# Index keys loaded as 2 KB rows, the sample's pieces seven gathers apart, tile 0's value rows split by stage, one pair of heads routed ahead of the first gather

## The chip, the cores and the metric

The kernel runs on one core of one Trainium2 chip. The metric is the device time of one execution in microseconds (us), smaller is better. The engines are named as in the profile: PE (TensorE, with PEld for its weight loads), DVE (VectorE), ACT (ScalarE), POOL (GpSimd) and SP (SyncE). SP does no computing here: it issues the large loads to 16 shared DMA engines.

## What is computed

One step of a decoder layer, for a prompt of 528 rows (16 meta tokens and 512 tokens) and a sample group of 8 sequences with 8 new tokens each, in float32. The parts that matter here:

```python
# every token: one projection, then two attentions
I[t, s] = IDX_SCALE * sum_h w[t, h] * relu(q_idx[t, h] . k_idx[s])    # 4 heads of 64: the token indexer
sel     = top_k(I, 256)                                             # sample: over 2048 cached keys and 8 new ones
y_a     = attention(q_a, k_a[sel], v_a[sel])                        # sparse
y_b     = softmax(q_b . k_b / 8 + forget bias) @ v_b                # over all keys; the sample's lie in pages
h = LN1(ALPHA * x + w_out(sig(g_a) * (y_a @ W_a) + sig(g_b) * (y_b @ W_b)))
# product-key experts: 8 heads x 16 of 16384 experts for each token
pre  = u[expert] . h ;  coef = softmax(top) * gelu(pre) ;  out = sum coef * v[expert]
x = LN2(ALPHA * h + out)
```

The caches lie in pages of 128 keys, in a random order that a page table gives, 16 pages for each of the 8 sequences. Each expert row (u or v) has 1024 floats, 4 KB.

## The kernel before

The program has three phases, with a barrier of all engines after each of the first two. Phase 1 (`project`) makes the projection. Phase 2 (`prompt`) computes both attentions of the prompt, and with them, in step order (`merge_at`), the merge, the output projection and the first norm of tile 0 (the tiles of tokens for the experts are 0 to 3 for the prompt, 128 tokens each, and 4 for the 64 sample tokens). Phase 3 is everything else, and its order is a written plan.

**The plan.** The backbone is the list `gathers` (L434 to L447): 1152 indirect loads that POOL issues (L820). Each brings one expert row for each of 128 tokens, 512 KB, from `peer_u` (v = 0) or `peer_v` (v = 1) into one of 10 row buffers (16 from gather 750 on). Numbered from 0, the first 256 are tile 0's, u in 0 to 127 and v in 128 to 255; then 64 u rows of tile 1; from 320 on u and v of different tiles alternate. Before POOL issues gather n it waits until the row that was in this buffer (row n - 10) has been read. POOL issues in order, so one unread row holds all gathers behind it. Before every 32nd u row of a tile it waits for that pair of heads to be routed (`pair_routed`).

Every other piece of phase 3 is put at a gather number (`put(n, ...)`), and `plan` is the merged list. PE, ACT and DVE each walk through the same plan in order and do what is theirs. A row counts as work of the engine that reads it: all u rows are read by DVE (L1860, a multiply and sum); v rows either by DVE (L1867, L1869, scale and add) or by PE (L1214, products with a diagonal of coefficients that ACT makes in `spot`, L1512, four gathers ahead). `read_by_dve` (L449) says which: of tile 0's v rows three in four are DVE's, of tiles 1 to 3 one in eight.

What is placed around the change:
- `route` (L1794): for one tile and one pair of heads g, four stages on DVE that find the top 16 experts. For tile 0 the pairs g = 0 and 1 stand in `pre_items`, ahead of gather 0; g = 2 at gathers 4 to 16, g = 3 at 20 to 32.
- `merge_items(1)`: the merge and output projection of tiles 1 to 3 (gathers 0 to 112), their norms, then 16 `query` products on PE (L1069) at gathers 128 to 176, three gathers apart, and the key `score` products (L1081) up to gather 187.
- `sample_items` (L487), from gather 190 on: `ix` c (L1103, products of the index queries `qis` with the index keys of stage c: c = 0 to 3 are 512 keys of each sequence, c = 4 the new ones) and `iy` c (L1116, the weighted sum over heads). `ix` 0 is at gather 191, `iy` 0 at 194, and after a gap of 48 `ix` 1 at 242, `ix` 2 at 245, `ix` 3 at 250. Then eight rounds q of the sample's attention (q < 4 are the k_b, v_b rounds, q >= 4 the sparse ones), each with scores (L1150), a softmax (`s_max`, `s_exp`, `s_norm`, `s_turn`) and `s_weigh` (L1190), five gathers between pieces for q < 4. Beside them 32 `top` rounds on DVE (L1733) pick the 256 keys. They all end at gather 726; tile 4's merge ends at 806, and L548 asserts that this is below 830.
- SP's own order: `prompt` (L681) issues stores and the first merge weights; `first_merges` the weights of `query`; `sample` (L718) the index keys (128 loads, stage 0 of all sequences first, then after `sc_ready` 16, the last key scores, stages 1 to 3 sequence by sequence), then the pages of k_b, v_b and kv_a into a ring of four slots, each when its slot has been read. Page numbers come from a table in SBUF (`page_numbers`), so SP also runs register instructions between the loads.

The index keys of one page are 64 rows (one per feature) of 128 keys:

```python
            sp.dma_start(ring[s_][p0:p0 + 64, at + j % 4 * 128:at + (j % 4 + 1) * 128],   # L730: 64 rows of 512 B
```

so that `ix` contracts over 128 partitions, two sequences at a time, and the queries of a sequence must stand on its 64 partitions in `qis`. DVE copies them there with 16 small copies and the new keys with 2 (L1602 to L1615) at the end of phase 1.

## Time and profile before

| | us |
|---|---|
| median of 3 runs | 2494.94 (2492.96 to 2496.37) |
| the profiled execution | 2496.61 |
| its span, first to last instruction | 2494.8 |
| PE busy | 1870.8 (75%) |
| DVE busy | 1664.1 (67%) |
| POOL busy | 1344.5 (54%) |
| ACT busy | 433.0 (17%) |
| granted TensorE clock, mean | 0.879 |

The core's DMA engines moved 791.69 MB, 604.58 MB of them on POOL's queue (the gathers) and 180.59 MB on the queue of SP and ACT. The first gather is issued at 466.9 us, the last at 2474.3 us. Times below count from the first instruction. "Releaser" in brackets is what ended an engine's idle time. "DMA share" is the mean busy share of the 16 DMA engines; the trace shows values up to 1.04 where they are full. A row of windows gives start:end and length, the busy time and number of instructions of PE, PEld, DVE, ACT and POOL, then the granted clock, the DMA share and GB/s.

### The profile page before, as it was taken

The page shows a single profiled execution, that of the slowest core. Times are in us where ns is not written, and L with a number is a line of the kernel's source. Part 1 is how long each engine was busy: PE and PEld are TensorE (multiplying, and loading weights), DVE is VectorE, ACT ScalarE, POOL GpSimd, SP SyncE. Part 2 cuts the span into 40 slices and gives each one's busy share as a digit, 9 for nine tenths or more (in the row PEclk, how much of TensorE's full clock was granted, in tenths as well). Part 3 has the DMA queues.
Part 4 walks back from the last instruction along what each step waited for, and adds up shares of the span by engine and source line. Part 5 has one row for each costly group of instructions (what it writes and reads, how often), then busy time and mean ns, then how long its engine had stood idle before and what let it go on. Part 6 is the DMA issues. An engine that isn't in the chain of part 4 may idle for free. (4 is left out here: it accounts for less than half of the span.)

```text
span 2494.8 us, 23480 instructions
## 1 busy us (share of the span) xinstructions
PE 1870.8 (75%) x6566; PEld 909.3 (36%) x6566; DVE 1664.1 (67%) x3371; ACT 433.0 (17%) x1052; POOL 1344.5 (54%) x1174
## 2 busy tenths in 40 slices
PE   8999998979759736326767677667678986667686
PEld 6756644735335412102222223233234542222231
DVE  2114886798784997987997575489555469745544
ACT  0123533101011201101111022122121121111110
POOL 1100000357755656655445467756767668877775
PEclk9998987989979868659887899889889998899999
DMA  4205330889989989999999999989999999899997
GB/s 182 63 12 168 96 119 9 314 319 386 409 293 340 317 253 385 402 396 348 377 381 350 367 381 380 390 326 358 400 405 409 409 397 344 332 372 410 408 394 294
DMA packets 258180, 791.69 MB, mean 317 GB/s; under 512 B 30562, under 2 KB 55203, under 8 KB 257347
## 3 DMA queue, kind: packets, MB, share of 16 engines
q0 software_dynamic: 166400, 604.58, 63.4%
q1 hardware_dynamic: 90692, 180.59, 20.6%
q10 hardware_dynamic: 960, 5.03, 0.5%
q8 instruction: 54, 0.88, 0.1%
q14 instruction: 74, 0.61, 0.1%
HBM read 783.90 MB, written 5.59 MB: 316 GB/s over the span
## 5 line engine op out<-in xcount | busy, mean ns | idle before, releaser
L1214 PE MATMUL ps<-arena 128*128 128x512 f32 (+1 forms) x1600 | 845.4, 664 | 310.5 <-DMA arena<-peer_v,arena 263.5
L820 POOL DMA_INDIRECT arena<-peer_u,arena x576 | 671.9, 1167 | 610.5 <-DVE arena L1823 317.7
L1860 DVE CUSTOM_DVE_ANT_0 arena<-arena 128x1024 f32<-128x1024 f32 x576 | 694.0, 1226 | 394.3 <-DMA arena<-peer_u,arena 385.7
L820 POOL DMA_INDIRECT arena<-peer_v,arena x576 | 653.2, 1134 | 390.0 <-PE ps L1214 178.0
L1214 PEld LDWEIGHTS ps<-arena 128*128 128x128 f32 (+1 forms) x1600 | 300.0, 203 | 798.6 <-issue 628.0
L1869 DVE SCALAR_TENSOR_TENSOR arena<-arena 128x1024 f32<-128x1024 f32 x171 | 219.9, 1286 | 128.9 <-DMA arena<-peer_v,arena 124.1
L1512 ACT ACTIVATE arena<-arena 128x128 f32<-128x128 f32 (+1 forms) x400 | 149.4, 394 | 728.5 <-PE ps L1214 725.1
L1037 PE MATMUL ps<-arena 128*128 128x448 f32 (+2 forms) x512 | 158.0, 468 | 22.6 <-DVE arena L1763 21.9
L1069 PE MATMUL ps<-arena 128*128 128x128 f32 (+2 forms) x768 | 149.4, 354 | 3.0 <-ACT arena L1400 3.0
L849 PE MATMUL ps<-arena 128*128 128x296 f32 (+1 forms) x512 | 130.7, 415 | 10.5 <-DMA arena<-w_proj 10.5
L1190 PE MATMUL ps<-arena 128*64 128x512 f32 (+1 forms) x512 | 90.7, 501 | 61.3 <-DMA arena<-v_b 61.3
L1069 PEld LDWEIGHTS ps<-arena 128*128 128x128 f32 x768 | 111.1, 198 | 44.4 <-issue 10.4
L1037 PEld LDWEIGHTS ps<-arena 128*128 128x128 f32 x512 | 89.4, 194 | 95.8 <-issue 79.8
L849 PEld LDWEIGHTS ps<-arena 128*128 128x128 f32 (+1 forms) x512 | 95.8, 188 | 43.8 <-issue 12.1
L1150 PE MATMUL ps<-arena 128*32 128x512 f32 x256 | 47.7, 881 | 81.3 <-DMA arena<-k_b 73.2
L804 POOL DMA_INDIRECT arena<-logf_b,arena x16 | 14.6, 912 | 129.6 <-PE ps L849 129.6
L1190 PEld LDWEIGHTS ps<-arena 128*64 128x64 f32 x512 | 36.3, 150 | 122.4 <-issue 121.7
L1733 DVE MAX8 arena<-arena 64x8 f32<-64x2056 f32 x32 | 73.6, 2300 | 1.2
L885 PE MATMUL ps<-arena 64*128 64x384 f32 (+9 forms) x168 | 70.5, 529 | 3.7 <-ACT arena L1376 1.9
L1734 DVE MATCH_REPLACE8 arena<-arena 64x2056 f32<-64x2056 f32 x32 | 73.1, 2286 | 0.0
L1049 PE MATMUL ps<-arena 128*128 128x512 f32 (+1 forms) x128 | 56.7, 596 | 1.8 <-DVE arena L1763 1.8
L1168 PE MATMUL ps<-arena 128*128 128x128 f32 x128 | 23.7, 362 | 42.3 <-ACT arena L1471 42.2
(192 smaller groups left out, 1648.7 us busy)
## 6 DMA issues: line engine op xcount, KB each, us to landing
arena<-k_b SPq DMA_DIRECT2D x128, 256.0 KB, 20.8
arena<-v_b SPq DMA_DIRECT2D x128, 256.0 KB, 15.4
arena<-w_mix SPq DMA_DIRECT2D x56, 512.0 KB, 6.7
arena<-w_q SPq DMA_DIRECT2D x48, 512.0 KB, 6.6
arena<-kv_a SPq DMA_DIRECT2D x128, 128.0 KB, 15.1
arena<-w_out SPq DMA_DIRECT2D x24, 512.0 KB, 6.7
arena<-peer_u,arena POOLq DMA_INDIRECT x576, 9.1
arena<-peer_v,arena POOLq DMA_INDIRECT x576, 6.8
```

The lines of the kernel that those rows point to most:

```text
L820: pool.indirect_dma_start(out=rows[slot_of[n]], out_offset=None, in_=io["peer_v"] if v else io["peer_u"], in_offset=bass.IndirectOffsetOnA ...
L849: last = pe.matmul(bank(2 * (m % 2) + a, HT, 0, n), wring[m % 3][:, k, 0:n], xT[:, k, a * HT:(a + 1) * HT], start=(k == 0), stop=(k == KD ...
L885: last = pe.matmul(out, heads[0:rows_, q, q0:q0 + nq], heads[0:rows_, kt, c0:c1], start=True, stop=not biased)
L1037: last = pe.matmul(out, mw_k[u % NMW][:, k0 + k, :], src[:, k, :], start=(k == 0), stop=(k == nk - 1))
L1069: last = pe.matmul(bank(4 + n % 2, WIDTH[p]), mw_k[u % NMW][:, k, :], hT[p][:, k, :], start=(k == 0), stop=(k == KD - 1))
L1190: last = pe.matmul(out[e], probT_s[:, c, j * 128 + 64 * e:j * 128 + 64 * e + 64], rhs, start=(c == 0 and j == 0), stop=False)
L1214: last = pe.matmul(bank(6 + a, 512, 0, nt), diag_p[read_before[n] % ND][:, 0:nt], rows[slot_of[n]][:, a * 512:(a + 1) * 512], start=(k == ...
L1512: act.activation(diag_p[r_ % ND][:, 0:nt], place, ACT.Copy, scale=coef[i % 2][:, k:k + 1]).then_inc(dp_ready, 1)
L1733: step(dve.max(top8, isamp))
L1734: step(dve.match_replace(isamp, top8, isamp, TAKEN))
L1860: dve.tensor_tensor_reduce(out=row, in0=row, in1=h, scale=1.0, scalar=0.0, op0=ALU.mult, op1=ALU.add, accum_out=pre[:, k:k + 1]).then_inc( ...
L1869: ins = dve.scalar_tensor_tensor(facc, row, c, facc, ALU.mult, ALU.add)
```

## The change

It makes five edits.
1. `kidx` pages are loaded as 16 rows of 2 KB (4 features of 128 keys each) onto 16 partitions of a sequence. `ix` then contracts over 64 partitions, four sequences at a time, in four accumulating steps r, so it has 8 matmuls for each c instead of 4.
2. The queries and new keys for that form no longer come from DVE's copies. SP stores them to DRAM (5 stores, pieces of 32 B) in phase 2, ahead of its stores of v and k, waits for that, and loads them back with 16 small loads ahead of the fifth merge weight.
3. Tile 0's v rows: k < 16 three in four on DVE as before, k = 16 to 63 all on DVE, k = 64 to 127 every second on DVE (92 rows on DVE instead of 96).
4. Tile 0's routing: only pair 0 ahead of gather 0; pair 1 at gathers 2 to 11, pair 2 at 16 to 28, pair 3 at 34 to 46; the gate at 52 and 56, and `gelu` and `coefs` of tile 0 not before 57 and 60.
5. Sample plan: the gap after `iy` 0 is 22 instead of 48 (`ix` 1 at gather 216, `ix` 2 at 219, `ix` 3 at 224, `ix` 4 at 229); pieces of q < 4 seven gathers apart instead of five; the gap after `s_out` for q >= 3 is 8 instead of 16. The sample's part ends at gather 738, tile 4's merge at 818.

```diff
@@ -335,11 +335,12 @@
         idx_added, mask_ready, weights_ready = sem("idx_added"), sem("mask_ready"), sem("weights_ready")
         pt_ready, pt_copied = sem("pt_ready"), sem("pt_copied")
         o_ready, o_copied = sem("o_ready"), sem("o_copied")
-        spread_a, spread_d = sem("spread_a"), sem("spread_d")
+        spread_a = sem("spread_a")
         wrow_spread, wd_ready = sem("wrow_spread"), sem("wd_ready")
         lidx_ready, lp_loaded, lf_ones = sem("lidx_ready"), sem("lp_loaded"), sem("lf_ones")
         g0_ready, g0_copied, sig0_done = sem("g0_ready"), sem("g0_copied"), sem("sig0_done")
         b0_ready, b0_mixed, ln0_loaded = sem("b0_ready"), sem("b0_mixed"), sem("ln0_loaded")
+        qsc_stored, qsc_loaded = sem("qsc_stored"), sem("qsc_loaded")
         ix_ready, ix_read, iy_ready, iy_read = (sem(n) for n in ("ix_ready", "ix_read", "iy_ready", "iy_read"))
         tail_new = sem("tail_new")
         masks_ready, rows_loaded = sem("masks_ready"), sem("rows_loaded")
@@ -363,6 +364,7 @@
         folded = sem("folded")
 
         csc = nc.dram_tensor("neg_cumulative", [NH, T], F32, kind="Internal").ap()
+        qsc = nc.dram_tensor("index_of_sample", [64, NB, NI + 1, SN], F32, kind="Internal").ap()
 
         def col(j, w=1, p=128, p0=0):
             return small[p0:p0 + p, j:j + w]
@@ -452,7 +454,7 @@
             if i == 4:
                 return k % 2 == 0
             if i == 0:
-                return k % 4 != 3
+                return k % 4 != 3 if k < 16 else k < 64 or k % 2 == 0
             return k % 8 == 5
 
         by_dve = [read_by_dve(*g) for g in gathers]
@@ -485,22 +487,22 @@
             return out
 
         def sample_items():
-            out = [(("zero",), 0), (("spread", 0), 1), (("ix", 0), 3), (("iy", 0), 48), (("ix", 1), 3)]
+            out = [(("zero",), 0), (("spread", 0), 1), (("ix", 0), 3), (("iy", 0), 22), (("ix", 1), 3)]
             for c in range(2, 5):
                 out += [(("ix", c), 2), (("iy", c - 1), 3)]
             out += [(("iy", 4), 2), (("admit",), 1)]
-            out += [(("s_score", 0, c), 5) for c in range(5)]
+            out += [(("s_score", 0, c), 7) for c in range(5)]
             out += [(("s_max", 0), 2), (("s_exp", 0), 2), (("s_norm", 0), 2), (("s_turn", 0), 3)]
             for q in range(NB):
                 if q + 1 < NB:
                     out.append((("spread", q + 1), 0))
-                g = 5 if q < 4 else 3
+                g = 7 if q < 4 else 3
                 if q < 3:
                     for c in range(5):
-                        out += [(("s_score", q + 1, c), 5), (("s_weigh", q, c), 5)]
+                        out += [(("s_score", q + 1, c), 7), (("s_weigh", q, c), 7)]
                 else:
                     out += [(("s_weigh", q, c), g if c < 4 else 1) for c in range(5)]
-                    out += [(("s_out", q), 16)]
+                    out += [(("s_out", q), 8)]
                     if q + 1 < NB:
                         out += [(("s_score", q + 1, c), 3) for c in range(5)]
                 if q + 1 < NB:
@@ -509,12 +511,13 @@
             return out
 
         pre_items = [item for item, _ in merge_items(0)]
-        pre_items += [("route", 0, g, s_) for g in range(2) for s_ in range(4)]
+        pre_items += [("route", 0, 0, s_) for s_ in range(4)]
         for s_ in range(4):
-            put(4 + 4 * s_, "route", 0, 2, s_)
-            put(20 + 4 * s_, "route", 0, 3, s_)
-        put(38, "gate_in", 0)
-        put(42, "gate", 0)
+            put(2 + 3 * s_, "route", 0, 1, s_)
+            put(16 + 4 * s_, "route", 0, 2, s_)
+            put(34 + 4 * s_, "route", 0, 3, s_)
+        put(52, "gate_in", 0)
+        put(56, "gate", 0)
 
         at = 0
         for item, gap in merge_items(1):
@@ -554,8 +557,8 @@
             for g in range(-(-rows_of[i] // 32)):
                 k1 = min(32 * g + 32, rows_of[i])
                 n = gather_at[i, 0, k1 - 1]
-                put(max(n + 3, 44 if i == 0 else 0), "gelu", i, g)
-                put(max(n + 6, 47 if i == 0 else 0), "coefs", i, g)
+                put(max(n + 3, 57 if i == 0 else 0), "gelu", i, g)
+                put(max(n + 6, 60 if i == 0 else 0), "coefs", i, g)
         for n, (i, v, k) in enumerate(gathers):
             if not by_dve[n]:
                 put(max(n - 4, gather_at[i, 0, min(32 * (k // 32) + 32, rows_of[i]) - 1] + 7), "spot", n)
@@ -684,17 +687,28 @@
                                  csc[:, LP + b * SN:LP + (b + 1) * SN]).then_inc(tail_new, 16)
                 for w in range(NMW):
                     weights(w)
+                for h in range(NI + 1):
+                    sp.dma_start(qsc[:, :, h, :], heads[0:64, QI + h, LP:T].rearrange("p (b t) -> p b t", t=SN)
+                                 ).then_inc(qsc_stored, 16)
                 for i, (t0, nt) in enumerate(TILES):
                     sp.dma_start(io["v_out"][t0:t0 + nt, :], vtm[0:nt, i, :]).then_inc(v_stored, 16)
                 sp.dma_start(io["k_out"][:, 0:2, :], heads[0:64, KA:KA + 2, :]).then_inc(k_stored, 16)
                 sp.dma_start(io["k_out"][:, 2:3, :], heads[0:64, KI:KI + 1, :]).then_inc(k_stored, 16)
                 sp.dma_start(io["k_out"][:, 3:11, :], heads[0:64, KB:KB + NH, :]).then_inc(k_stored, 16)
                 x_rows(0)
+                sp.wait_ge(qsc_stored, 16 * (NI + 1))
+                for b in range(NB):
+                    c0 = b % 4 * 32
+                    of_b = qsc.rearrange("(p r) b h t -> b p r h t", r=4)[b]
+                    sp.dma_start(qis[16 * b:16 * b + 16, :, c0:c0 + 32], of_b[:, :, 0:NI, :].rearrange("p r h t -> p r (h t)")
+                                 ).then_inc(qsc_loaded, 16)
+                    sp.dma_start(kin[16 * b:16 * b + 16, :, :], of_b[:, :, NI, :]).then_inc(qsc_loaded, 16)
                 for w in range(NMW, first_query + NMW):
                     weights(w)
                     if w == weight_no["out", 0, NMW, 0]:
                         for dst, l in ((lng0, 0), (lnb0, 1)):
                             sp.dma_start(dst, io["ln"][l:l + 1, :].partition_broadcast(128)).then_inc(ln0_loaded, 16)
+                sp.wait_ge(qsc_loaded, 16 * 2 * NB)
                 sp.wait_ge(k_stored, 16 * 3)
                 sp.wait_ge(tail_new, 16 * NB)
 
@@ -724,12 +738,11 @@
                         sp.wait_ge(mix_done, KD)
                     for b in range(NB):
                         nos = page_numbers(b * NPG + 4 * c0, 4 * (c1 - c0))
-                        p0, at = 64 * (b % 2), b // 2 * 512
                         for j, no in enumerate(nos):
                             s_ = c0 + j // 4
-                            sp.dma_start(ring[s_][p0:p0 + 64, at + j % 4 * 128:at + (j % 4 + 1) * 128],
-                                         io["kidx"].rearrange("(n d) k -> n d k", d=64)[bass.ds(no, 1)].rearrange(
-                                             "o d k -> (o d) k")).then_inc(ring_loaded[s_], 16)
+                            sp.dma_start(ring[s_][16 * b:16 * b + 16, j % 4 * 512:(j % 4 + 1) * 512],
+                                         io["kidx"].rearrange("(n p r) k -> n p (r k)", p=16, r=4)[bass.ds(no, 1)].rearrange(
+                                             "o p x -> (o p) x")).then_inc(ring_loaded[s_], 16)
                 for z, (kind, q, c, e) in enumerate(fill_list):
                     s_ = z % NSLOT
                     if kind == "ki":
@@ -1097,12 +1110,14 @@
                 if c >= 2:
                     pe.wait_ge(ix_read, 2 * (c - 1))
                 w = 512 if c < 4 else SN
-                keys = unit("ki", -1, c, 0).rearrange("p (a n) -> p a n", a=4) if c < 4 else kin
-                for g in range(2):
-                    for p in (2 * g, 2 * g + 1):
-                        last = pe.matmul(bank(2 * (c % 2) + g, w), qis[:, p, :], keys[:, p, :], start=(p % 2 == 0),
-                                         stop=(p % 2 == 1))
-                    last.then_inc(ix_ready, 1)
+                keys = unit("ki", -1, c, 0).rearrange("p (j r k) -> p r j k", j=4, r=4) if c < 4 else kin
+                for r_ in range(4):
+                    for g in range(2):
+                        p0 = 64 * g
+                        last = pe.matmul(bank(2 * (c % 2) + g, w), qis[p0:p0 + 64, r_, :], keys[p0:p0 + 64, r_],
+                                         start=(r_ == 0), stop=(r_ == 3))
+                        if r_ == 3:
+                            last.then_inc(ix_ready, 1)
                 if c < 4:
                     pe.wait_ge(ix_ready, 2 * c + 2)
                     pe.sem_inc(slot_read, 1)
@@ -1599,20 +1614,6 @@
                 for g in range(NKV):
                     dve.tensor_copy(qac[64 * g:64 * g + 64], heads[0:64, QA + 4 * g:QA + 4 * g + 4, LP:T])
                     dve.tensor_copy(kan[64 * g:64 * g + 64, :], heads[0:64, KA + g, LP:T])
-                dve.wait_ge(zero_set, 1)
-                for h in range(NI):
-                    for e in range(2):
-                        for pp in range(2):
-                            c0 = (2 * pp + e) * 32 + h * 8
-                            dst = qis.rearrange("p (a b) c -> p a b c", b=2)[64 * e:64 * e + 64, :, pp, c0:c0 + 8]
-                            src = heads[0:64, QI + h, LP:T].rearrange(
-                                "p (a b e t) -> p a b e t", b=2, e=2, t=SN)[:, :, pp, e, :]
-                            dve.tensor_copy(dst, src)
-                for e in range(2):
-                    last = dve.tensor_copy(
-                        kin[64 * e:64 * e + 64, :, :],
-                        heads[0:64, KI, LP:T].rearrange("p (a e t) -> p a e t", e=2, t=SN)[:, :, e, :])
-                last.then_inc(spread_d, 1)
 
             norms = [0]
```

## Rows read from the trace of the kernel before

**Rows 1.** Windows of the span: busy time, then PEclk, DMA share, GB/s.

```profile
467.00:590.00 123.00, 105.03 (x303) 56.15 (x302) 115.44 (x310) 14.47 (x32) 78.69 (x63) 0.93 0.93 345
...
730.00:835.00 105.00, 104.37 (x348) 60.54 (x347) 59.30 (x88) 15.77 (x36) 58.94 (x54) 1.00 0.97 349
835.00:940.00 105.00, 50.99 (x99) 18.93 (x97) 100.93 (x245) 11.46 (x29) 65.55 (x51) 0.70 0.86 278
940.00:1110.00 170.00, 75.91 (x263) 25.45 (x263) 148.96 (x192) 20.30 (x39) 112.65 (x90) 0.68 1.04 398
1110.00:1200.00 90.00, 61.27 (x203) 23.81 (x201) 68.04 (x150) 16.41 (x36) 40.91 (x38) 0.87 0.92 344
...
1300.00:1420.00 120.00, 78.45 (x251) 28.42 (x251) 77.98 (x101) 18.52 (x40) 55.94 (x50) 0.77 0.93 346
```

**Rows 2.** What POOL waited for, 730 to 835 us: total, times, longest.

```profile
POOL arena L820 <- PE ps L1214: 33.6, 13, 7.2
```

**Rows 3.** What POOL waited for, 835 to 940 us.

```profile
POOL arena L820 <- DVE arena L1869: 27.5, 12, 4.1
```

**Rows 4.** From the page's costliest groups: busy us, mean ns | idle before.

```profile
L1869 DVE SCALAR_TENSOR_TENSOR arena<-arena 128x1024 f32<-128x1024 f32 x171 | 219.9, 1286 | 128.9 <-DMA arena<-peer_v,arena 124.1
```

**Rows 5.** Timeline of DVE: first and last instruction of one routed pair.

```profile
450.99 0.49 DVE L1783 MAX8 arena<-arena 128x8 f32<-128x128 f32 x2 [24.31 <-ACT arena L1414]
...
465.97 0.20 DVE L1823 SCALAR_TENSOR_TENSOR arena<-arena 128x32 uint32<-128x32 f32 x1
```

**Rows 6.** Gathers of line L820: from issue to landing.

```profile
DMA to landing us min/median/max: 4.2/7.6/24.1
```

**Rows 7.** Timeline of PE: start us, us, what [idle before <-releaser].

```profile
820.42 1.88 PE L1214 MATMUL ps<-arena 128*128 128x512 f32 x4
...
844.03 3.68 PE L1103 MATMUL ps<-arena 128*128 128x512 f32 x8 [2.50 <-DMA arena<-kidx]
...
949.20 5.10 PE L1103 MATMUL ps<-arena 128*128 128x512 f32 x8 [3.92 <-DMA arena<-kidx]
```

**Rows 8.** Timeline of SP's queue: all index key loads; those of stages 1 to 3.

```profile
802.97 145.76 SPq L730 DMA_DIRECT2D arena<-kidx  x128
...
845.87 102.86 SPq L730 DMA_DIRECT2D arena<-kidx  x96
```

**Rows 9.** SP's issues by line: ns min/median/max, first and last start.

```profile
L730 SPq DMA_DIRECT2D arena<-kidx x128: 468/469/602, 803.0 to 948.3; - x128
...
L743 SPq DMA_DIRECT2D arena<-k_b x128: 332/333/2527, 952.7 to 1374.5; - x128
...
L683 SPq DMA_DIRECT2D arena<-neg_cumulative x8: 263/295/298, 201.5 to 203.9; - x8
```

**Rows 10.** Windows of line L820 alone: x is the number of gathers issued.

```profile
466.00:881.50 415.50, 263.48 (x216) 0.90 0.94 344
466.00:909.00 443.00, 279.52 (x228) 0.89 0.93 339
466.00:962.00 496.00, 314.69 (x257) 0.87 0.93 336
```

**Rows 11.** What PE waited for, 940 to 1850 us.

```profile
PE ps L1150 <- DMA arena<-k_b: 73.2, 9, 16.2
PE ps L1190 <- DMA arena<-v_b: 61.3, 11, 11.0
```

**Rows 12.** SP's DMA queue, 835:940 and 1000:1080: packets, MB, share.

```profile
q1 hardware_dynamic: 7134, 2.93, 11.5%
...
q1 hardware_dynamic: 5587, 10.18, 33.8%
```

**Rows 13.** What DVE waited for at the first barrier: us, times, longest.

```profile
DVE arena L1633 <- PEq L636: 35.0, 1, 35.0
```

**Rows 14.** Timeline of SP's queue in the prompt phase.

```profile
212.43 21.92 SPq L671 DMA_DIRECT2D arena<-w_mix  x6
```

**Rows 15.** Timeline of PE there: the product with the fifth merge weight.

```profile
228.70 5.29 PE L904 MATMUL ps<-arena 128*128 128x128 f32 x32
```

## The prediction, made before the changed kernel was run

> **What bounds the kernel now.** I read the windows of the span first. From the first gather on, the DMA engines are the common bound: where they are full their share is 1.04, and a window below that holds idle DMA time of (1.04 - share) x length [rows 1]. That gives 13.5 us in 467 to 590, 7.4 in 730 to 835, 18.9 in 835 to 940, none in 940 to 1110, 10.8 in 1110 to 1200 and 13.2 in 1300 to 1420. Only such time can be won: the bytes of the gathers do not change. Next I asked who left the engines idle. In 730 to 835 POOL waits 33.6 us for rows that PE has not read, and PE is busy 104 of 105 us [rows 1, 2]: the `query` products stand in its path. In 835 to 940 POOL waits 27.5 us for DVE's reads, DVE is busy 101 of 105 us, and PE half the time [rows 1, 3]. A read of a v row costs DVE 1.29 us [rows 4].
>
> **Routing pair 1 behind gather 0: 0.** The first gather waits for pair 0 alone in both kernels. Routing a pair takes DVE 15.2 us [rows 5]. Before, pair 1 fills the time in which the first rows land; behind the change DVE waits for them, some 6 us (a gather lands 4.2 us after its issue at best, 7.6 in the median [rows 6]), and the work of pair 1 still comes. DVE is busy 115 of 123 us here [rows 1], so this is a loss. The gain is that the last pair ends at gather 46 instead of 32: fourteen more rows are asked for sooner, while DVE reads (1.29 us) faster than full DMA engines deliver (90 gathers in 170 us, 1.9 us each [rows 1]), worth at most 14 x 0.6 = 8 us. I take 0, with -8 and +7 as ends.
>
> **Rows 144 to 191 all on DVE.** A row costs PE 1.88 us [rows 7]. Eleven PE rows (147, 151, up to 187) go before the last key score: -21 us of PE's path, of which at most the window's 7.4 us of idle DMA time is gained on the gathers. DVE has room: 59 of 105 us busy [rows 1], and twelve reads more are 15 us. **Rows 192 to 255 half on DVE.** DVE, the bound of 835 to 940, loses nine reads (rows 193 to 225), 9 x 1.29 = 12 us, within that window's 18.9 us. So far this is a gain of up to 19 us at gather 256, if nothing else stands there.
>
> **The index keys: where it goes wrong.** Something does stand there: `ix` 1 moves from gather 216 + 26 = 242 to 216, and PE, which walks the plan in order, waits in it until stage 1 of the keys has landed. Before, it waits only 3.9 us, until 949.2 us [rows 7]. When will they land now? SP issues the 128 loads in an unbroken run of 145.8 us, the 96 of stages 1 to 3 in 102.9 us [rows 8], so 1.07 us a load, of which the load instruction itself is 0.47 [rows 9]; the rest is register work for page numbers, which the change keeps. The loads interleave the stages, so stage 1 ends about when the whole does. The new load (16 rows of 2 KB) has no row. Its issue lies between 0.26 us, the least of the 8-row loads, and 0.47, today's; nearest in kind is 0.33, rows of 2 KB too [rows 9]. With 0.33, 0.14 us a load is saved. The start: four of PE's eleven removed rows stand ahead of the query that lets SP begin, -7 us; 32 loads of stage 0, -4.5; and SP no longer waits 2 us for the last key score: -13 in all. Then 88 loads to the end of stage 1, -12. Stage 1 lands at 949.2 - 25 = 924 us (915 with 0.26, 940 with 0.47).
>
> But row 215 was issued just before 881.5 us [rows 10] and comes no later now; I take 870 and landing at 876. From there PE stands still for 48 us. Half of the v rows from 192 on are now PE's, so row 217 stays unread, and gather 227, which takes its buffer, is held, with all behind it. DVE's removed work gains nothing then. After 924 PE runs `ix` 1. Today's four matmuls take 3.7 us, or 5.1 at a lower clock [rows 7]; eight take 7.4 to 10 if each costs the same, I take 9; then row 217, and gather 227 goes out at about 935. Before, 228 gathers were out by 909 [rows 10]: 27 us late. The next 29 take 53 us before (257 by 962 [rows 10]). Now the DMA engines start empty, but `ix` 2 and 3 (7.4 us each) stand between the next PE rows: I take 51 us. So gather 256 is 25 us late, with 16 and 41 from the two issue costs, and everything after it shifts. The 7 and 12 us above are in this, not beside it.
>
> The doubled matmuls are the uncertain piece within it. The Trainium skill (TensorEngine Tiling, Theoretical Speedup) has a contraction of 64 or less run up to twice as fast in two row tiles, and the two halves here use different partitions. By that rule `ix` stays at 3.7 to 5.1 us and the total would be some 4 us lower than by the row; no row here shows two such halves side by side.
>
> **Seven gathers between pieces.** Between 940 and 1850 PE waits 73.2 us for k_b and 61.3 us for v_b [rows 11], and while it waits its v rows hold POOL. A piece consumes 2 MB. SP's queue gets a share of 0.34 of the engines beside full gathers [rows 12], about 127 GB/s, so five gathers (5 x 1.9 us, from 90 gathers in 170 us [rows 1]) bring 1.2 MB and seven 1.7 MB: PE waits less. But while PE waits the loads themselves keep the engines busy, so the 134 us of waiting are worth only the idle DMA time of those windows, 10.8 + 13.2 us, and part of that is the softmax turn between rounds, which stays. I take half of the sum and less for the later rounds: -11 us, ends 0 and -24. The shorter gap after `s_out` fits in work that stays full: 0.
>
> **2 KB rows.** Keys in 512 B rows: 2.93 MB in 0.115 x 105 = 12.1 us of all engines, 243 GB/s. k_b in 2 KB rows: 10.18 MB in 0.338 x 80 = 27 us, 377 GB/s [rows 12]. 4.19 MB of keys take 17 us and would take 11. These 6 us fall into the stall, so they are 0 here; if there is no stall they count.
> The Trainium skill (DMA: Bandwidth & Descriptors, Specifications) gives 512 B as the least transfer at line rate; by that the 6 us don't exist, against the rows here.
>
> **The detour of the queries.** DVE's 18 copies lie in front of a barrier at which DVE waits 35.0 us for PE [rows 13]: removing them gains 0. SP's queue in phase 2 gets five stores of 512 pieces of 32 B (0.26 to 0.6 us each by the issues shown [rows 9], more if the pieces count, for which there is no row), a wait until they have landed (4 us, as the quickest gather [rows 6]), and 16 small loads of 0.26 to 0.47 us: 10 to 15 us together. All of it stands ahead of the fifth merge weight, issued at 212.4 us [rows 14]: it goes out at 222 to 227 and lands 4 to 8 us later [rows 6], 226 to 235. PE begins with it at 228.7 us [rows 15]. PE is busy most of that phase, so I count +4 us, ends 0 and +10. If a whole step's slack covers it, it costs nothing.
>
> **The sum** is made against the profiled execution: 2496.6 + 0 + 25 - 11 + 4 = 2514.6 us. The median of the runs is 1.7 us below that execution, so I predict **2513 us**. A difference of 0.2%, 5 us, is about what a measurement of this kernel can tell from none.
>
> **Rivals.**
> *No real stall (faster).* If SP issues a 16-row load in well under 0.26 us, stage 1 lands near 900 us, gather 227 is about on time, and the relief of PE and DVE shows: -7 and -12 us in the two windows, -6 for the packets, at most -25 in all. For it: sixteen descriptors rather than 64. Against it: the quickest load of the rows takes 0.26 us, and the register work alone keeps SP busy for 102.9 - 96 x 0.47 = 58 us. A half of the 25, -12, gives 2496.6 - 12 - 11 + 4 - 1.7 = 2476 us. The point of decision is stage 1 landing before or after about 905 us.
> *The stall is real, the sample stage pays it back.* With pieces balanced against the queue's share, all 24 us of idle time in 1110 to 1420 go: 2496.6 + 25 - 24 + 4 - 1.7 = 2500 us. Against it stands the softmax turn, for which PE waits on ACT and DVE whatever the spacing.
> *Everything at its dear end.* Issue stays at 0.47 us, the detour costs 10 us and the spacing gives 5: 2496.6 + 41 + 10 - 5 - 1.7 = 2541 us.
>
> **Chances.** Forecast 0.46, no real stall 0.26, paid back 0.16, dear end 0.12. Faster than 2490: the first rival and a little of the second, 0.29. Within 5 us: most of the second's lower side, 0.10. Slower: 0.61. The range runs from 2474 (about a third of the first rival lies below) to 2540 (half of the dear end above).
>
> **What would show it.** PE's wait for kidx in front of `ix` 1 grows from 3.9 us to tens, ending near 924; POOL shows one long wait released by PE there, and 228 gathers are out only after 930. SP's load of keys has a new issue time. In phase 2 the product with the fifth merge weight begins after 228.7. PE's waits for k_b and v_b fall well below 134 us. I am wrong if gather 256 goes out before 962 us: then the keys came sooner, or PE's rows did not hold POOL.

## The result, and the profile after

The changed kernel takes 2533.68 us (median of 4 runs, 2530.48 to 2539.17), the kernel before, beside it, 2495.65 us (2492.96 to 2501.88): a ratio of 1.0159, 95% interval 1.0132 to 1.0187. It is 38 us slower; 18 were forecast. The profiled execution of the changed kernel took 2539.17 us with a span of 2537.4.

The windows first, the same stretches as [rows 1]. Columns: length, then busy us (and instructions) of PE, PEld, DVE, ACT and POOL, then PEclk, DMA share, GB/s.

```profile
467.00:590.00 123.00, 107.87 (x386) 63.46 (x386) 111.23 (x323) 11.07 (x32) 70.40 (x56) 0.96 0.95 350
730.00:835.00 105.00, 103.14 (x368) 63.22 (x368) 72.33 (x80) 18.29 (x35) 71.14 (x60) 0.97 0.96 346
835.00:940.00 105.00, 46.68 (x90) 16.71 (x90) 92.42 (x261) 9.21 (x25) 45.67 (x37) 0.69 0.85 247
940.00:1110.00 170.00, 92.04 (x335) 32.36 (x335) 126.96 (x158) 24.26 (x48) 115.09 (x90) 0.75 1.01 381
1110.00:1200.00 90.00, 53.47 (x143) 18.60 (x142) 72.15 (x137) 8.87 (x22) 52.46 (x44) 0.80 1.00 385
...
1300.00:1420.00 120.00, 88.47 (x266) 30.86 (x264) 89.00 (x115) 21.98 (x51) 73.17 (x68) 0.91 1.03 400
```

835 to 940 is the stretch of the index keys: 37 POOL instructions where there were 51, and 247 GB/s where there were 278. Further on, 1110 to 1200 and 1300 to 1420 are better than before (1.00 and 1.03 against 0.92 and 0.93): by the prediction's measure, (1.04 - share) x length, idle DMA time there falls from 24 us to 5. What lies behind the stretch that the prediction looked at is worse. The two kernels from 1500 to 1960 us, the sample's rounds 4 to 7 (`kv_a` rows) and their surroundings, first before, then after:

```profile
1500.00:1960.00 460.00, 344.15 (x1092) 142.43 (x1091) 284.35 (x614) 87.17 (x212) 329.76 (x289) 0.89 1.00 383
```

```profile
1500.00:1960.00 460.00, 315.46 (x1056) 133.48 (x1055) 273.91 (x581) 91.88 (x222) 285.01 (x250) 0.85 0.94 349
```

By the same measure idle DMA time there is 18 us before and 46 us after. These 28 us are the largest loss of any stretch; with the first gather 12 us later and the 19 us won from 1110 to 1420 they make up part of the 38. The windows stand at fixed times and hold different work in the two kernels, so this is no exact account.

PE's timeline at the keys, as [rows 7]: start, duration, what, and in brackets the idle time before it.

```profile
899.23 1.96 PE L1229 MATMUL ps<-arena 128*128 128x512 f32 x4 [1.51 <-DMA arena<-peer_v,arena]
931.14 6.60 PE L1117 MATMUL ps<-arena 64*128 64x512 f32 x16 [29.96 <-DMA arena<-kidx]
938.09 1.96 PE L1229 MATMUL ps<-arena 128*128 128x512 f32 x4 [0.34 <-PE ps L1117]
939.97 3.72 PE L1117 MATMUL ps<-arena 64*128 64x512 f32 x16
```

And POOL there, one long wait released by PE:

```profile
912.27 1.86 POOL L833 DMA_INDIRECT arena<-peer_v,arena  x1 [1.67 <-DVE arena L1870]
940.32 0.94 POOL L833 DMA_INDIRECT arena<-peer_v,arena  x1 [26.19 <-PE ps L1229]
```

SP's queue, as [rows 8 and 9]: the 128 key loads as one run, and their issue time in ns.

```profile
808.00 125.74 SPq L743 DMA_DIRECT2D arena<-kidx  x128
```

```profile
L743 SPq DMA_DIRECT2D arena<-kidx x128: 315/316/751, 808.0 to 933.4; - x128
```

Every part of the forecast stall is here: PE waits 30.0 us for `kidx`, until 931 (924 forecast), and the new issue costs 0.316 us (0.33 forecast). The stall is shorter than the forecast 48 us, because PE still had rows to read until 901 and not only until 876: gather 215 went out at 891.4 us, where the prediction took 870. Gather 256 goes out at 990.1 us against 961.6: 28.5 us late, where stall and detour together were forecast at 29.

The prompt phase, SP's queue, as [rows 14]: the detour's stores, what follows them, its loads (14 more of 0.6 us between the last two lines), and the fifth merge weight.

```profile
208.76 5.06 SPq L691 DMA_DIRECT2D index_of_sample<-arena  x5
213.86 3.15 SPq L694 DMA_DIRECT2D v_out<-arena  x5
...
220.77 2.39 SPq L703 DMA_DIRECT2D arena<-index_of_sample  x1
223.20 2.62 SPq L705 DMA_DIRECT2D arena<-index_of_sample  x1
...
234.98 25.28 SPq L674 DMA_DIRECT2D arena<-w_mix  x10
```

PE's product with that weight, as [rows 15]:

```profile
238.95 6.26 PE L917 MATMUL ps<-arena 128*128 128x128 f32 x32 [10.54 <-DMA arena<-w_mix]
```

It starts 10.3 us later than before, and gather 0 goes out at 479.1 instead of 466.9: 12.2 us, where 4 were forecast.

Last, what PE waited for from 1500 to 1960 us, before and after (in all, times, longest):

```profile
PE ps L1158 <- DMA arena<-kv_a: 10.6, 3, 4.2
```

```profile
PE ps L1173 <- DMA arena<-kv_a: 67.6, 7, 16.0
```

This wait was in no step of the prediction. So two stories stood against each other: the loss at the end is that of gather 256 carried on (detour and keys), or that one was paid back and the rounds of 4 to 7 cost anew, by `s_out`'s gap of 8 or by the spacing of seven, which puts these rounds beside tile 3's routing.

### The profile page after: what moved, and what is told of

The parts are those of the page before. It is cut to its first block, busy times and chain, and to the rows that moved or that the text cites. A ratio compares the mean times of both kernels' runs of the same rounds, so it can differ in the third digit from the quotient of the medians.

```text
span 2537.4 us, 23595 instructions
## 1 busy us (share of the span) xinstructions
PE 1872.6 (74%) x6622; PEld 909.3 (36%) x6622; DVE 1654.6 (65%) x3349; ACT 434.3 (17%) x1056; POOL 1353.8 (53%) x1174
## 4 chain that ended last, share of the span: by engine, by line
DMA 17%; PE 13%; POOL 10%; SPq 6%; issue 5%; DVE 1%; ACT 1%; ACTq 0%; DVEq 0%
POOL arena L833 10%; PE ps L1229 8%; DMA arena<-peer_v,arena 7%; SPq L763 4%; DMA arena<-v_b 3%; DMA arena<-kv_a 3%; DMA arena<-peer_u,arena 2%; DMA arena<-k_b 2%; PE ps L1205 2%; SPq L681 1%; PE ps L1082 1%; SPq L756 1%; PE ps L1183 1%; PE ps L1165 0%; PE ps L1173 0%
## 5 line engine op out<-in xcount | busy, mean ns | idle before, releaser
L1229 PE MATMUL ps<-arena 128*128 128x512 f32 (+1 forms) x1616 | 839.7, 656 | 280.7 <-DMA arena<-peer_v,arena 239.0
L833 POOL DMA_INDIRECT arena<-peer_v,arena x576 | 662.3, 1150 | 382.8 <-PE ps L1229 164.3
L1870 DVE SCALAR_TENSOR_TENSOR arena<-arena 128x1024 f32<-128x1024 f32 x167 | 214.7, 1286 | 138.9 <-DMA arena<-peer_v,arena 134.8
L862 PE MATMUL ps<-arena 128*128 128x296 f32 (+1 forms) x512 | 131.6, 418 | 10.6 <-DMA arena<-w_proj 10.6
L1205 PE MATMUL ps<-arena 128*64 128x512 f32 (+1 forms) x512 | 96.0, 524 | 48.6 <-DMA arena<-v_b 48.6
L1173 PE MATMUL ps<-arena 128*64 128x512 f32 x64 | 22.7, 793 | 67.6 <-DMA arena<-kv_a 67.6
L1165 PE MATMUL ps<-arena 128*32 128x512 f32 x256 | 39.3, 739 | 41.1 <-DMA arena<-k_b 39.9
L1710 DVE TENSOR_REDUCE arena<-ps 128x1 f32<-128x128 f32 (+4 forms) x68 | 32.8, 500 | 43.5 <-PE ps L902 37.6
```

What stands on the lines that cost most here:

```text
L833: pool.indirect_dma_start(out=rows[slot_of[n]], out_offset=None, in_=io["peer_v"] if v else io["peer_u"], in_offset=bass.IndirectOffsetOnA ...
L862: last = pe.matmul(bank(2 * (m % 2) + a, HT, 0, n), wring[m % 3][:, k, 0:n], xT[:, k, a * HT:(a + 1) * HT], start=(k == 0), stop=(k == KD ...
L1205: last = pe.matmul(out[e], probT_s[:, c, j * 128 + 64 * e:j * 128 + 64 * e + 64], rhs, start=(c == 0 and j == 0), stop=False)
L1229: last = pe.matmul(bank(6 + a, 512, 0, nt), diag_p[read_before[n] % ND][:, 0:nt], rows[slot_of[n]][:, a * 512:(a + 1) * 512], start=(k == ...
L1870: ins = dve.scalar_tensor_tensor(facc, row, c, facc, ALU.mult, ALU.add)
```

## The experiments

They ran in four sets, on different chips, on which the same kernel before took 2546.94, 2538.08, 2496.96 and 2551.91 us. So the sets are compared by ratios to it.

### First set: the changed kernel with parts undone

The detour's stores and loads moved behind the seventh and the ninth merge weight, where SP waits for PE anyway:

```diff
                 for w in range(NMW, first_query + NMW):
                     weights(w)
+                    if w == NMW + 2:
+                        for h in range(NI + 1):
+                            sp.dma_start(qsc[:, :, h, :], heads[0:64, QI + h, LP:T].rearrange("p (b t) -> p b t", t=SN)
+                                         ).then_inc(qsc_stored, 16)
+                    if w == NMW + 4:
+                        sp.wait_ge(qsc_stored, 16 * (NI + 1))
+                        for b in range(NB):
...
```

> The changed kernel with the stores of the sample's index heads and the loads back issued among the merge weights of the prompt (after the seventh and the ninth weight), not ahead of v_out, k_out and the fifth weight. Theory (the detour's 12.1 us at gather 0 come from SP's queue ahead of the fifth weight, and stay to the end): the product behind the fifth weight is back at about 229 us, gather 0 at 467 and the time 2533.7 - 12 = about 2522 us. Rival (gather 0 comes earlier, but the stalls behind it swallow it, as they are set by plan and bytes): gather 0 at 467 and the time within 4 us of 2533.7. Second rival (the routing behind gather 0 is what moved it): gather 0 stays at 479.

Measured: ratio 1.0076 (1.0045 to 1.0107). Gather 0 is at 467.3, so SP's queue is the cause of its lateness, and the routing is not. In the trace the 12 us melt away, as the rival has it. Against the next two runs, with the early detour on the same chip, it is 7 and 4 us ahead at gather 128 (713.9 us, and 720.5 and 717.6), and 3 and 0 at gather 240 (968.7, and 972.0 and 968.5). PE's longest wait for `kidx` is 40.9 us here and 41.3 and 37.1 in those two. By ratios, 1.0159 and 1.0076, 21 us came back, with an uncertainty of about 10. The two readings do not agree, and this pair alone doesn't settle the detour's price.

The gaps of the plan, one after the other (numbers: index tail, piece spacing, `s_out`; the change has 22, 7, 8):

```diff
-            out += [(("s_score", 0, c), 7) for c in range(5)]
+            out += [(("s_score", 0, c), 5) for c in range(5)]
-                g = 7 if q < 4 else 3
+                g = 5 if q < 4 else 3
-                        out += [(("s_score", q + 1, c), 7), (("s_weigh", q, c), 7)]
+                        out += [(("s_score", q + 1, c), 5), (("s_weigh", q, c), 5)]
```

> The changed kernel with the sample's pieces five gathers apart again; s_out stays at 8 and the index tail at 22. Theory (s_out's gap is a cost of 20 to 30 us, the spacing of seven a gain of about 11): 2533.7 + 11 = about 2545 us, with PE's wait for kv_a again at 60 us or more. Rival (the late end of the sample's stage, 39 gathers behind, is what the spacing costs: its rounds of sequences 4 to 7 now meet the routing of tile 3): clearly under 2533.7, about 2510 us, and the wait for kv_a at about 10 us.

```diff
-                    out += [(("s_out", q), 8)]
+                    out += [(("s_out", q), 16)]
```

> The changed kernel with the pieces five apart and s_out at 16, as before the change; only the index tail stays at 22, with the 2 KB keys, the detour, the routing and tile 0's split. Theory: against the run with s_out at 8 it is 20 to 30 us faster, so about 2520 us, and PE's wait for kv_a falls from 60 to 70 us to about 10. Rival (s_out's gap is worth nothing, the waits for kv_a belong to transfers that are bound by bytes anyway): within 5 us of the run with s_out at 8.

```diff
-(("iy", 0), 22)
+(("iy", 0), 48)
```

> The changed kernel with all gaps of the plan as before (index tail 48, pieces 5, s_out 16): what is left of the change is the 2 KB keys with their detour, the routing behind gather 0 and tile 0's split. Theory (the 30 us wait for kidx at the 64-row product comes from the gap of 22 alone): PE's wait for kidx in that stage is back under 8 us, gather 256 is some 17 to 25 us earlier than with 22, and the time is about 2500 us (2495 + 12 for the detour - 7 for the split). Rival (the 2 KB keys themselves cost, by their doubled products or by their rows): within 6 us of the run with 22, 5 and 16.

Measured: 22, 5, 8 has a ratio of 1.0189 (1.0127 to 1.0252); 22, 5, 16 has 1.0050 (1.0009 to 1.0090); 48, 5, 16 has 1.0008 (0.9970 to 1.0047). The step of `s_out` is by far the largest, 33.7 us between medians on one chip (2591.74 and 2558.07), a little over what was expected. What PE waited for from 1500 to 1960 us, with 8, and then with 16:

```profile
PE ps L1173 <- DMA arena<-kv_a: 53.8, 6, 16.3
```

```profile
PE ps L1173 <- DMA arena<-kv_a: 24.5, 3, 11.0
```

The rival for the spacing falls: undoing the seven did not make the kernel faster. The index tail is a surprise. With 22, gather 256 was 12.6 us later than with 48 (992.2 and 979.6; 17 to 25 were expected), but gather 848 went out at 2079.2 and 2078.5, and the spans are 2556.3 and 2555.6. The medians differ by 11.4 us, with intervals that overlap. The profiled execution with 48 was itself 11 us above its median and the one with 22 was not, so the two traces may hide that much. The tail's price at the end is 10 us with an uncertainty of 14: not resolved from zero, and smaller than the 25 forecast at gather 256. The run with 48 missed its expectation in one more thing: a wait of 18.5 us for `kidx` was left, where under 8 had been expected.

### Second set: parts of the change alone, and the change again

The changed kernel itself, unedited:

> The changed kernel itself, once more, beside the others of this set. Theory: 1.6% over the kernel before here as well; against the run with the pieces five apart (ratio 1.0189) the spacing of seven is a gain of 5 to 15 us. Rival (the spacing is worth nothing or costs, and 1.0159 and 1.0189 differ by the chips they came from): 1.019 or more here.

Measured: 1.0168 (1.0093 to 1.0243), a second reading of 1.0159. Against 1.0189 the spacing of seven is a gain of some 7 us, inside the intervals' width. Up to gather 464 it looks far larger, 1391.8 us here and 1436.4 with five, on two different chips; at gather 720 it is 1879.2 and 1899.9. Most of the lead is lost again by the end.

The kernel before, with `s_out` at 8 and nothing else:

```diff
-                    out += [(("s_out", q), 16)]
+                    out += [(("s_out", q), 8)]
```

> The kernel before with one number changed: s_out's gap 8 instead of 16 (index tail 48, pieces 5, keys in 512 B rows). Theory (the gap is the change's dearest part: eight gathers fewer per round leave SP and the DMA queues too little time for a round's key and value rows of sequences 4 to 7): 20 to 35 us slower than before, a ratio of 1.008 to 1.014, PE's wait for kv_a from 10.6 to 50 us or more. Rival (the gap costs only together with the later start of these rounds in the changed plan, where they meet the routing of tile 3): within 5 us of before.

Measured: 1.0043 (1.0019 to 1.0067), 11 us. The wait is what the theory said, the time about half of it:

```profile
PE ps L1158 <- DMA arena<-kv_a: 63.4, 8, 16.9
```

So the gap costs by itself: 11 us with an uncertainty of 6, and 35 with one of 19 beside the changed plan's other gaps. Whether it really costs more there, and why, stays open; no run separates it.

The kernel before with the 2 KB keys, their detour late, and tile 0's split; routing and gaps as before. The edits are those of the change and the move above.

> The kernel before with the 2 KB keys, the detour issued late and tile 0's split; routing and all gaps as before (48, 5, 16). Theory (the detour's place costs 12 us, the keys nothing, the split gains up to 7): gather 0 at 467, gather 128 before 708, and a ratio of 0.995 to 1.000. Rival (the gain at gather 128 is taken back by the wait for kidx, as the index stage's loads can't start earlier than the merge of the pass before allows): gather 128 some 7 us earlier, gather 320 and the end as before, ratio 1.000.

The kernel before with the split alone:

```diff
             if i == 0:
-                return k % 4 != 3
+                return k % 4 != 3 if k < 16 else k < 64 or k % 2 == 0
```

> The kernel before with tile 0's split alone (VectorE takes the rows of its first stage up to number 63, then every second one). Theory: gather 176 is 7 to 12 us earlier than before, as POOL waits less for PE between gathers 128 and 176, and the time is 5 to 10 us shorter (ratio 0.996 to 0.998). Rival (PE's relief there is swallowed by the wait for the index keys' landing, which does not move with it): gather 256 and the time as before, within 0.2%.

Measured: 0.9973 (0.9947 to 1.0000) and 1.0000 (0.9972 to 1.0027). These two belong together. For the first, gather 128 was expected before 708 and came at 709.7. With the split alone gather 176 goes out at 792.9 us, 15 us before that of the run with `s_out` at 8 alone on the same chip (808.4), and gather 256 at 967.0, only 6 before (972.9): PE arrives sooner at keys that land hardly sooner. For the time the rival holds: nothing was gained. Its waits for `kidx` from 840 to 990 us:

```profile
PE ps L1103 <- DMA arena<-kidx: 35.9, 2, 19.6
```

With the 2 KB keys as well there is no such wait in that stretch, and gather 256 is at 955.7. SP's key loads, first with the split alone, then with the 2 KB keys:

```profile
799.35 155.77 SPq L730 DMA_DIRECT2D arena<-kidx  x128
```

```profile
798.70 132.04 SPq L744 DMA_DIRECT2D arena<-kidx  x128
```

The run of the key loads is 24 us shorter with 2 KB rows. SP's issue time accounts for most of that, 128 x (0.469 - 0.316) = 20 us, and the DMA engines for none of it. This is SP's queue in the changed kernel from 835 to 940 us (packets, MB, share), where [rows 12] have 2.93 MB in 12.1 us of all engines, 243 GB/s:

```profile
q1 hardware_dynamic: 3453, 3.66, 15.5%
```

That is 16.3 us for 3.66 MB, 225 GB/s (the keys and four first loads of k_b). In time the gain over the split alone is not resolved (0.9973 and 1.0000 overlap), and no run has the 2 KB keys without the split. In the changed kernel the shorter tail asks for the keys 26 gathers (some 50 us) sooner, which is more than that.

### Third and fourth set: the same levers, turned the other way

All four build on the base of `keys_split_late_detour`: the 2 KB keys, the detour late and tile 0's split. `s_out`'s gap widened to 20; the spacing at six with tail 40 and `s_out` 14; the changed routing added; and, alone in its set, `s_out` at 22 with tail 40.

```diff
-                    out += [(("s_out", q), 16)]
+                    out += [(("s_out", q), 20)]
```

> The kernel before with the 2 KB keys, the detour late, tile 0's split, index tail 48, pieces 5, and s_out's gap 20 instead of 16 (the run of this base with 16 had a ratio of 0.9973). Theory (a round of sequences 4 to 7 is bound by its rows' landing, and the gap is what it lasts): the wait for kv_a falls from 14.3 us to under 5, ratio 0.993 to 0.997. Rival (at 16 the rounds are no longer bound by their rows; a wider gap only moves the end of the stage nearer to the merge of tile 4): ratio 0.997 to 1.001.

> The same base with the index tail at 40, the pieces six gathers apart and s_out at 14, the widest spacing for which merge and routing of tile 4 still fit. Theory (by the changed kernel against the one with pieces five apart, some 44 us earlier at gather 464 and 7 to 12 at the end: a spacing gain that is paid back later only in part): waits for k_b and v_b fall by a third, ratio 0.992 to 0.997 if the two gathers less for s_out cost under 5 us. Rival (only moved in time, as gathers and key and value rows share the DMA engines): 0.997 to 1.003.

> The same base with s_out at 16 and the changed routing (first rows gathered behind one pair of heads): the changed kernel with all gaps as before and the detour late. Against keys_only_gap48 (ratio 1.0008) this moves only the detour; against keys_split_late_detour (0.9973) only the routing. Theory: the routing is worth nothing (0 of -8 to +7), so 0.9973 within 0.3%, and the detour's place 12 us at gather 0 of which at most 9 reach the end. Rival (routing pair 1 and the later gates cost at gathers 48 to 128 what the earlier gather 0 gave): ratio 1.000 or more, with gather 128 over 6 us behind keys_split_late_detour.

```diff
-(("iy", 0), 48)
+(("iy", 0), 40)
-                    out += [(("s_out", q), 16)]
+                    out += [(("s_out", q), 22)]
```

> The same base (2 KB keys, detour late, tile 0's split, the routing of before) with s_out at 22 and, to make room in the plan, the index tail at 40 instead of 48; the run with 20 and 48 had a ratio of 0.9907. Theory (s_out's gap pays until the wait for kv_a is gone, which was 7.3 us at 20; a tail of 40 is still behind the keys' landing, as with pieces six and tail 40 no wait for kidx stood in the trace): wait for kv_a under 5 us, ratio 0.987 to 0.992. Rival (no more to gain at 20; later rounds only press on the merge of tile 4): ratio 0.991 to 0.997.

| tail, spacing, `s_out` | routing | ratio | 95% | PE's wait for kv_a, us |
|---|---|---|---|---|
| 48, 5, 16 | before | 0.9973 | 0.9947 to 1.0000 | 14.3 |
| 48, 5, 16 | changed | 0.9960 | 0.9939 to 0.9981 | 14.1 |
| 40, 6, 14 | before | 0.9946 | 0.9923 to 0.9970 | 33.7 |
| 48, 5, 20 | before | 0.9907 | 0.9871 to 0.9943 | 7.3 |
| 40, 5, 22 | before | 0.9872 | 0.9844 to 0.9901 | none |

The wait goes with `s_out`'s gap: 22, 20, 16, 14 give none, 7.3, 14 and 33.7 us in the table. Over all traces 16 gives 10.6 to 24.5, and 8 gives 53.8 to 71.3 in all five runs that have it. The window from 1500 to 1960 us with 20:

```profile
1500.00:1960.00 460.00, 344.09 (x1099) 143.06 (x1098) 283.99 (x613) 90.10 (x215) 338.49 (x297) 0.91 1.01 388
```

297 POOL instructions, against 289 before and 250 after. Beyond 16 there was more to gain, so that rival falls: 20 has 0.9907, and 16 on the same chip 0.9960. Beyond 20 it is not shown: 0.9907 and 0.9872 overlap in their intervals, and the tail was changed with it. The wait at 20 was expected under 5 us and was 7.3. The routing makes no difference that can be told, as expected (0.9960 against 0.9973, on two chips). The detour's place can be read at this base as well: 1.0008 with it early, 0.9960 with it late, all else the same. That is 12 us, with an uncertainty of about 11 from the two intervals; gather 256 moves from 979.6 to 956.0, though part of that is a wait of 19.5 us of POOL for DVE that only the first of these runs shows before its keys. Six gathers between pieces, with two fewer for `s_out` and a shorter tail, reads 3 to 7 us better than five, not resolved. Its expectation failed in the waits for k_b and v_b, which were to fall by a third: they are 128.1 us (81.0 and 47.1), against 122.2 (57.4 and 64.8) with five on the same chip. The last version, 0.9872, beats both kernels: some 32 us under the kernel before and 72 under the changed one, each as its ratio times 2495.65 us.

## Why the prediction was right or wrong

The ratios form a chain, from the second row on with one edit between neighbours; times 2495.65 us each:

| step | ratio | term | forecast |
|---|---|---|---|
| 2 KB keys, split, routing; detour late | 0.9960 | -10 | 0 |
| detour early | 1.0008 | +12 | +4 |
| tail 48 to 22 | 1.0050 | +10 | +25 |
| `s_out` 16 to 8 | 1.0189 | +35 | 0 |
| spacing 5 to 7 | 1.0159 | -7 | -11 |
| sum | | +40 | +18 |

The first term is uncertain by 5 us; the intervals of neighbours combine to about 11, 14, 19 and 17 us for the others. So `s_out`'s and the first stand clear of zero, the detour's barely, the other two don't. The neighbours often ran on different chips, and another order of the steps might share the sum out otherwise. Without `s_out` the terms come to +5 where +18 was forecast: the errors in them hid a part of the 35.

**Direction and place of the stall: right.** PE stood at `ix` 1 until 931, POOL behind it, gather 227 out at 940.3 (935 forecast), gather 256 28.5 us late (29 forecast). The waits for k_b and v_b fell, 134.5 us to 88.5 (39.9 and 48.6). That gather 256 came out within 1 us of the forecast is partly luck. The keys' loads began at 808.0 us, 5 later than before and not 7 earlier, and stage 1 was there at 931 and not 924. On the other side, the stall began later and was shorter, and the detour's 12 us had shrunk to 2 by gather 192 (837.2 us, 835.1 before), where the relief of PE counts as well.

**The step that failed is the sentence "The shorter gap after `s_out` fits in work that stays full: 0".** It was worth 35 us here, 11 alone. The prediction held what was needed to price it. It had SP's queue at about 127 GB/s beside full gathers, and used that for the pieces only. A round of 4 to 7 takes 32 loads of 128 KB, 4.19 MB, into slots that the weighing of the round before frees; at 127 GB/s that is an estimated 33 us. A gap of 8 gathers lasts about 15 us (1.9 each), one of 16 about 30. SP's queue before, in the four rounds, then after:

```profile
1476.29 34.38 SPq L750 DMA_DIRECT2D arena<-kv_a  x32
...
1554.92 39.57 SPq L750 DMA_DIRECT2D arena<-kv_a  x32
...
1650.27 28.00 SPq L750 DMA_DIRECT2D arena<-kv_a  x32
...
1739.93 34.59 SPq L750 DMA_DIRECT2D arena<-kv_a  x32
```

```profile
1542.50 37.96 SPq L763 DMA_DIRECT2D arena<-kv_a  x32
...
1628.75 39.58 SPq L763 DMA_DIRECT2D arena<-kv_a  x32
...
1710.63 39.24 SPq L763 DMA_DIRECT2D arena<-kv_a  x32
...
1795.15 38.06 SPq L763 DMA_DIRECT2D arena<-kv_a  x32
```

And PE's first and third score in one of the rounds, before and after:

```profile
1695.29 1.08 PE L1158 MATMUL ps<-arena 128*64 128x512 f32 x4
...
1703.87 1.08 PE L1158 MATMUL ps<-arena 128*64 128x512 f32 x4
```

```profile
1661.20 1.98 PE L1173 MATMUL ps<-arena 128*64 128x512 f32 x4 [3.46 <-DMA arena<-kv_a]
...
1683.68 1.97 PE L1173 MATMUL ps<-arena 128*64 128x512 f32 x4 [11.20 <-DMA arena<-kv_a]
```

In this round the first score comes 45.0 us after the loads began before (1695.3 - 1650.3), and 32.5 us after (1661.2 - 1628.8); it is the round with the largest difference. Over the four rounds the first score comes 37.0, 42.7, 45.0 and 38.3 us behind the first load before, and 35.5, 32.5, 32.1 and 30.9 after: 8 us sooner in the mean. The third score comes no sooner, 53.7 us in the mean before and 55.8 after. So by this reading the loads set its time, and what the plan saves in gathers PE spends in waiting. While PE waits, its unread rows hold POOL: POOL's waits for PE in 1500 to 1960 rose from 32.5 to 100.3 us.

The price shows in how long a gather takes. From the first load of round 4 to that of round 7, POOL issues 158 gathers in 263.6 us before, 1.67 us each, and 135 in 252.7 us after, 1.87 each. That is 27 us over three of the four rounds. The traces of all runs agree: 1.83 to 1.93 us a gather with a gap of 8, 1.64 to 1.71 with 16, 1.69 with 14, 1.60 with 20 and 1.61 with 22. The kernel before with 8 alone has 1.84 there, 18 to 20 us more than the two runs with 16 on its chip (1.71 and 1.69), though only 11 show in its time.

**The detour: mechanism right, size off.** +4 forecast, 12 at gather 0, and 12 by the table above, barely resolved. The loads were costed at 0.26 to 0.47 us, by rows with other shapes; they took 0.59 us each and 2.4 and 2.6 for the first two, 14.2 us together, and the stores 5.1. The fifth weight left at 235.0, not 222 to 227, and the 12 us at gather 0 lie past the end that the range allowed (+10).

**The stall: right where it stands, probably too dear at the end.** "Everything after it shifts" is not borne out: in the two traces with 22 and 48 no difference was left by gather 848, and by the medians it is 11 us, with an uncertainty of 14. The tail's 26 gathers also bring the whole sample stage forward; that this pays the stall back is argued and not shown.

**"The 7 and 12 us above are in this": right** for the change as made, as far as `before_split` shows: relief ahead of the keys' landing lengthened the wait for them, and the time stayed the same.

**2 KB rows: the rate was taken from a load of another shape.** The keys were to take 11 us of the engines and not 17, at the 377 GB/s of k_b. In the window 835 to 940 they moved at 225 GB/s, no faster than in 512 B rows, so the 6 us do not exist. The forecast had them at 0 and is not touched; the first rival counted them.

**Doubled matmuls: the rule, not the row.** 16 records of 64 rows take 3.72 us in the row at 939.97, and today's 8 of 128 rows 3.68 [rows 7], both at a granted clock of 1.00; 9 us were taken. By the rule that stood beside it (the Trainium skill, TensorEngine Tiling, Theoretical Speedup) 3.7 to 5.1 was given, and the trace agrees. The first stage, behind PE's wait of 30 us, took 6.60 us at a mean granted clock of 0.57, so mostly at the lower of the two levels.

**The spacing: nothing against it**, -7 against -11, but with an uncertainty of 17 the sign itself is not resolved. The rival "paid back" (2500 us) was half right, as early payback did come (gather 464 went out at 1384.4, 33.9 us earlier than before), and by gather 720 (1869.6 us, 31.4 later than before) the rounds of 4 to 7 had taken it again.

## What to carry to other kernels

A gap in a written order is a budget in time for a transfer. Price each one that an edit shortens: bytes that must land in it, over the queue's share when the other traffic runs, against the gap's length, times the number of rounds. Read the terms at the end of the kernel, not where they arise: a stall or a relief in the middle may be gone some hundred gathers on. A relief that comes before a fixed landing may be worth nothing until the landing moves too: here the split alone gave nothing, and split, faster keys and changed routing together 10 us. And take a transfer's rate from one of the same shape: the row size alone misled here.

## What the runs showed of the hardware

SP's issue time for a load depends on its shape in a way that bytes don't tell: 0.316 us for 16 rows of 2 KB, 0.333 for 128 rows of 2 KB [rows 9], 0.469 for 64 rows of 512 B [rows 9], and 0.59 for the detour's small loads, whose pieces are of 128 and 32 B. The rate on the DMA engines depends on more than the row size as well. Rows of 2 KB moved at 377 GB/s of engine time when they were k_b's, 128 rows onto 128 partitions [rows 12], and at 225 when they were the keys', 16 rows onto 16 partitions; keys in 64 rows of 512 B onto 64 partitions had 243. No run separates the number of rows, the partitions and the traffic beside them.

The five stores of 512 pieces of 32 B took 0.59 to 2.14 us each when issued early, and 11.8 us together in the late place.

Chips differ by more than the effects studied: the kernel before took 2495.65 to 2551.91 us in the five comparisons. The difference is in memory traffic as well. From 1960 to 2450 us, where the kernels run mostly gathers, the changed kernel shows this on the first chip, and then on that of the second set:

```profile
1960.00:2450.00 490.00, 364.75 (x970) 156.59 (x969) 291.27 (x616) 73.33 (x188) 364.92 (x332) 0.92 0.99 383
```

```profile
1960.00:2450.00 490.00, 351.46 (x932) 154.28 (x933) 287.48 (x617) 66.38 (x170) 356.93 (x320) 0.89 0.97 367
```
